# Weight block sums by accumulating DMAs in a seven-product feed-forward: two transformer blocks on one core

## What is computed

```python
def first_block(x, ...):
    ...
    x = x + jnp.einsum('btd,de->bte', mix, w_o[l])
    h = rmsnorm(x, ln2[l])
    gate, up = jnp.split(jnp.einsum('btd,df->btf', h, w_gu[l]), 2, axis=-1)
    x = x + jnp.einsum('btf,fd->btd', jax.nn.silu(gate) * up, w_down[l])
    return rmsnorm(x, ln_f)
```

## Time and profile before

| | us |
|---|---|
| three runs, median | 1124.53 (1123.28 to 1125.9) |
| the profiled execution | 1123.35 |
| its span, first to last instruction | 1121.5 |
| feed-forward, first gate matmul (228.80) to the end of the last down product (669.2) | 440.4 |

### The profile page before, as it was taken

One profiled execution on the slowest core, in us unless ns is written; L12 is line 12 of the kernel. 1 busy time (PEld: TensorE's weight loads), 2 busy tenths in 40 slices (PEclk: granted clock), 3 DMA queues, 4 the chain that ended last, 5 costly groups with the idle time before them and its releaser, 6 DMA issues.

```text
span 1121.5 us, 15711 instructions
## 1 busy us (share of the span) xinstructions
PE 1041.4 (93%) x5802; PEld 870.3 (78%) x5802; DVE 698.4 (62%) x1234; ACT 503.1 (45%) x945; POOL 486.8 (43%) x551
## 2 busy tenths in 40 slices
PE   9999999996777769998886999999999999999997
PEld 6887877775777768888886787876788777788886
DVE  6865666567566662346666685779965666425553
ACT  6432665543444442224444243645675555423333
POOL 1354533468566630046663343743353676541101
PEclk9999999997999999998888999999999999999999
DMA  8222332121222223312222333621132333233322
GB/s 281 87 76 76 96 88 84 57 77 37 76 76 76 75 90 117 94 58 75 75 76 76 113 102 104 222 77 57 58 88 83 95 113 113 75 95 94 94 75 75
DMA packets 34907, 102.51 MB, mean 91 GB/s; under 512 B 4608, under 2 KB 8128, under 8 KB 34832
## 3 DMA queue, kind: packets, MB, share of 16 engines
q1 hardware_dynamic: 34416, 100.99, 28.1%
q10 hardware_dynamic: 416, 0.52, 0.1%
HBM read 93.40 MB, written 4.74 MB: 88 GB/s over the span
## 4 chain that ended last, share of the span: by engine, by line
PE 64%; DVE 13%; POOL 9%; DMA 5%; issue 4%; ACT 4%; POOLq 0%; SPq 0%; DVEq 0%; ACTq 0%
PE bank L1684 16%; PE bank L1685 16%; PE bank L1686 16%; POOL WT L2629 8%; DMA WS<-wall 5%; PE bank L1848 2%; PE bank L1839 2%; DVE WL L2377 2%; DVE score L2490 1%; PE bank L1732 1%; PE bank L1734 1%; PE bank L1733 1%; DVE m L2488 1%; PE bank L1824 1%; ACT fs L2061 1%
## 5 line engine op out<-in xcount | busy, mean ns | idle before, releaser
L2580 POOL TENSOR_TENSOR WL<-WS,WH 128x256 fp32r<-128x256 f32 x272 | 219.8, 808 | 257.5 <-ACT WH L1901 240.4
L1684 PE MATMUL bank<-HH,WH 128*128 128x512 f32 x536 | 221.0, 412 | 10.1 <-DVE fa L2427 5.8
L1686 PE MATMUL bank<-HH,WL 128*128 128x512 f32 x536 | 211.6, 395 | 0.0
L1685 PE MATMUL bank<-HL,WH 128*128 128x512 f32 x536 | 211.4, 394 | 0.0
L1901 ACT ACTIVATE WH<-WS 128x1024 fp32r<-128x1024 f32 x122 | 126.4, 1047 | 36.6 <-PE bank L1686 34.5
L1698 PE MATMUL bank<-n_s,WH 128*128 128x256 f32 x304 | 92.4, 304 | 45.1 <-DVE WL L2377 33.8
L1684 PEld LDWEIGHTS bank<-HH,WH 128*128 128x128 f32 x536 | 102.5, 191 | 36.0 <-DVE fa L2427 6.2
L1686 PEld LDWEIGHTS bank<-HH,WL 128*128 128x128 f32 x536 | 101.9, 190 | 22.5
L1685 PEld LDWEIGHTS bank<-HL,WH 128*128 128x128 f32 x536 | 102.3, 191 | 19.2 <-issue 1.2
L2629 POOL TENSOR_TENSOR WT<-WS 128x256 f32<-128x256 f32 x76 | 68.2, 898 | 76.6 <-PE bank L1686 55.4
L1698 PEld LDWEIGHTS bank<-n_s,WH 128*128 128x128 f32 x304 | 60.9, 200 | 52.0 <-issue 33.7
(11 more groups left out here) (385 smaller groups left out, 2472.2 us busy)
## 6 DMA issues: line engine op xcount, KB each, us to landing
WS<-wall SPq DMA_DIRECT2D x161, 512.0 KB, 3.5
scratch<-rows SPq DMA_DIRECT2D x8, 320.0 KB, 5.1
b_t<-scratch SPq DMA_DIRECT2D x8, 256.0 KB, 3.6
X<-xT SPq DMA_DIRECT2D x7, 256.0 KB, 7.2
outT<-X SPq DMA_DIRECT2D x7, 256.0 KB, 2.4
b_m<-b_m SPq DMA_DIRECT2D x11, 128.0 KB, 2.2
f_s<-f_s SPq DMA_DIRECT2D x8, 128.0 KB
f_m<-f_m SPq DMA_DIRECT2D x8, 128.0 KB
```

The lines of the kernel that those rows point to most:

```text
L1684: e.matmul(b[:, :], wh, xh, start=k == 0, stop=False)
L1685: e.matmul(b[:, :], wh, xl, start=False, stop=False)
L1686: m = e.matmul(b[:, :], wl, xh, start=False, stop=k == n - 1)
L2580: e.tensor_tensor(WL[:, at_u, cs], WS[:, u % NST, cs], f32(WH[:, at_u, cs]), ALU.subtract).then_inc(*tick(w_low_g, u if c == 3 else (u, c)))
```

## The change

Four plain pairs instead of three, 18 pairs in the seven-product scheme instead of 19. The scheme is turned over (the roles of B11 and B22 change places): T1 = B22 + B12, T2 = T1 + B11, T4 = T2 + B21, T3 = B11 + B12. The sums are no longer made by POOL: a buffer `SS` of six blocks (128 x 512 each) is loaded by SP with B22, B11 and B21 from HBM (256 KB each, line 1627), and when a block's low half has been made, POOL issues a DMA (`b_add`, line 2682) that reads the next term from HBM and adds it into the same place in `SS`: B22 becomes T1, then T2, then T4; B11 becomes T3. That is three loads and four adding DMAs in each group; B11 and B12 are read from HBM twice. The `WS` ring now holds plain units alone, so units of the down product come in while the groups run. For plain pairs the low half of the weights moves from POOL to DVE (`now["low"] = w_low_g` goes). The product of gate and up in a group moves from POOL to DVE (`seven_mult`), and the `norm2` steps are spread one to a pair of tiles. `seven_step` puts steps of neighbouring groups beside each other: a group has places -9 to 12, the next begins seven places later, and each place has one of the seven products. The core of the diff:

```diff
-OLD_PAIRS = 3
+OLD_PAIRS = 4
+        SS = at("SS", [128, 6, 512], F32, place["at"])
-        WT = at("WT", [128, 2 * NW, 512], F32, WL_at)
...
-        def prepare(g, *names):
-            for name in names:
-                if name[-1] == "+":
-                    do("w_sum", g=g, name=name[:-1], before=block_at[g, name[:-1]][1])
-                else:
-                    do("w_block", g=g, name=name, before=block_at[g, name][1])
...
+        def make(g, name):
+            half = g[0]
+            while (g, name) not in block_at:
+                nxt = order_of[half].pop(0)
+                block_at[nxt] = slot(1, ("block", nxt))
+            do("w_block", g=g, name=name, before=block_at[g, name][1])
+            follower = {"B22": "T1", "T1": "T2", "T2": "T4", "B11": "T3"}.get(name)
+            if follower:
+                do("b_add", g=g, name=follower, after=name)
...
+        def group_at(g, x):
+            half, j = g
+            o = open_of.setdefault(g, {})
+            if x == -9:
+                do("b_load", g=g, name="B22")
+                do("b_load", g=g, name="B11")
+            elif x == -6:
+                make(g, "B11")
+            elif x == -5:
+                do("b_load", g=g, name="B21")
+            elif x == -4:
+                make(g, "B22")
+            elif x == -1:
+                make(g, "T1")
+            elif x == 0:
...
+                make(g, "B21")
+                o["yi"], o["y"], free = y_ring.take()
+                seven(g, "B11", "A11", o["y"], True, free)
+            elif x == 1:
+                do("partial", g=g, name="p", b=o["y"], dst=c_p)
+            elif x == 2:
+                make(g, "T2")
+                o["vi"], o["v"], free = t_ring.take()
+                seven(g, "B22", "s4", o["v"], True, free)
+            elif x == 3:
+                o["zi"], o["z"], free = s_ring.take()
+                seven(g, "T1", "s1", o["z"], True, free)
+            elif x == 4:
+                make(g, "T3")
+                seven(g, "T2", "s2", o["y"], False, partial((g, "p")))
+            elif x == 5:
+                do("partial", g=g, name="u2", b=o["y"], dst=c_u2)
+                make(g, "T4")
+                o["wi"], o["w"], free = t_ring.take()
+                seven(g, "B21", "A12", o["w"], True, free)
+            elif x == 6:
+                corner_of(g, "C11", o["w"], c_p)
+                t_ring.give(o["wi"], corner((g, "C11")))
+                seven(g, "T3", "s3", o["y"], False, partial((g, "u2")))
+            elif x == 7:
+                do("partial", g=g, name="u3", b=o["y"], dst=c_u3)
...
+            elif x == 8:
+                seven(g, "T4", "A22", o["z"], False, corner((g, "C22")))
+            elif x == 9:
+                corner_of(g, "C21", o["z"], c_u2)
...
+                do("seven_tanh", g=g)
+            elif x == 10:
+                do("seven_mult", g=g)
+            elif x == 11:
+                do("seven_hi", g=g)
+            elif x == 12:
+                do("seven_low", g=g)
...
-        now["low"] = w_low_g
...
+                elif kind == "b_load":
+                    g, name = s["g"], s["name"]
+                    n = groups.index(g)
+                    i = place_of(n, name)
+                    back, last = {"B22": (3, "T4"), "B11": (2, "T3"), "B21": (1, "B21")}[name]
+                    q.wait_ge(block_low((groups[n - back], last)) if n >= back else norm_a("n2"))
+                    e.dma_start(SS[:, i, :], wall_block(g, name)).then_inc(*block_in[i].tick((g, name)))
...
-                elif kind == "w_sum":
...
-                        e.tensor_tensor(WT[:, o, cs], src1[:, cs], src2[:, cs], ALU.add).then_inc(
-                            *tick(w_sum, (g, name) if c else (g, name, 0)))
+                elif kind == "b_add":
+                    g, name = s["g"], s["name"]
+                    i = place_of(groups.index(g), name)
+                    term = {"T1": "B12", "T2": "B11", "T4": "B21", "T3": "B12"}[name]
+                    q.wait_ge(block_low((g, s["after"])))
+                    e.dma_start(SS[:, i, :], wall_block(g, term), accum_op=ALU.add).then_inc(*block_sum[i].tick((g, name)))
```

More of the change, by code:

```diff
@@ L417, in tile @@
             plan.append(what)
-            while count["split"] <= min(t // UT + 2, NU - 1):
+            while count["split"] <= min(t // UT + 2, NU - 1) and not all(
+                    u in seven_of for u in range(count["split"], min(t // UT + 2, NU - 1) + 1)):
                 split()
@@ new lines, in seven_step @@
+        def seven_step(half, js, x):
+            if half not in order_of:
+                order_of[half] = [((half, j), name) for j in js for name in ("B11", "B22", "T1", "T2", "B21", "T3")]
+                for n, j in enumerate(js):
+                    order_of[half].insert(7 * n + (7 if n + 1 < len(js) else 6), ((half, j), "T4"))
+            for n in reversed(range(len(js))):
+                y = x - 7 * n
+                if y not in (7, 8):
+                    group_at((half, js[n]), y)
+                if n > 0 and y in (0, 1):
+                    group_at((half, js[n - 1]), y + 7)
@@ L1073, in build @@
                         next(up_gen)
-                    beside_old(gate_gen)
-                    beside_old(up_gen)
+                    for gen in (gate_gen, up_gen):
+                        for _ in gen:
+                            next(nh, None)
+                assert left == [0], left
                 run(nh)
-                js = js[OLD_PAIRS:]
-            now["low"] = w_low_v
-            for j in js:
-                seven_group((half, j), (half, j + 1) if j + 1 < FHS[half] else None)
+            js = of_half[half]
+            last = (half, js[-1])
+            for x in range(7 * len(js)):
+                seven_step(half, js, x)
+                if x == 7 * len(js) - 4 or x == 7 * len(js) - 1:
+                    split()
+            group_at(last, 7)
             if half == 1:
@@ L1509, in used @@
             return product_end(u) if kind == "block" else dense(unit_end.get(u, ("unit", u)))
[L1511 to L1518 removed]
+        plain = [u for u in range(NU) if u not in seven_of]
+        ring_of = {u: n % NST for n, u in enumerate(plain)}
+        groups = sorted(first_unit)
         def partial_free(g, name):
@@ L1550, in load @@
             def load(u):
-                while loads[0] <= min(u, NU - 1):
+                while loads[0] <= min(u, len(plain) - 1):
                     n = loads[0]
@@ L2055, in scalar_program @@
                     e.activation(NH[name][0][:, :, :].rearrange("p a n -> p (a n)"),
-                                 NF[:, NF_at[name]:NF_at[name] + 1024], ACT.Copy).then_inc(*norm2_a.tick(name))
+                                 NF[:, NF_at[name]:NF_at[name] + 1024], ACT.Copy,
+                                 scale=-1.0 if name == "A22" else 1.0).then_inc(*norm2_a.tick(name))
                 elif kind == "ffn_gate":
                     half, jj = s["half"], s["jj"]
-                    done = corner(((half, s["j"]), "C21")) if s["seven"] else out_v(("gate", jj))
```

318 lines of the change are left out of this document (142 added, 176 removed).

## The result

The changed kernel takes 1127.2 us (median of 13 runs, 1126.3 to 1129.1) where the kernel before takes 1124.05 in the same comparison: a ratio of 1.0030, 95% interval 1.0021 to 1.0038. It is a little slower. The prediction said 1092 and faster; the time lies in its range, on the other side of zero. The profiled execution has a span of 1126.9 us.

A forecast was written before the change was run, and what follows sets the result against it. Groups were bound by a ring of load, POOL sums, halves and load, 13.4 us each; the new ring costs 12.8. Front, groups, down products and seams end at 637.6 against 669.2: 31.6 less, 1091.8 us; range 1052 to 1136, forecast's own 1068 to 1119.

The forecast's parts named there:

- The loop: Group to group: T2's low half, C21, tanh, B22, T1, T2, two adds in series; 5.2 + 2A, 12.8 us.
- A: Time from a low half's end on DVE until ACT may read the adding DMA's sum; taken as 3.8 us.
- The second loop: Through tanh, two multiplications, result's high half and partial sum, one add: 8.3 + A; shorter once A is over 3.1.
- the prediction's own slope: Forecast total's change per microsecond of A: 2 + 16 x 2 = 34 us.
- The zero at A = 4.7: Value of A at which the forecast gain vanishes; above it the changed kernel would be slower.
- The rival with the slow add: At ACT's wait for `block_sum`: adding DMA slow; 1136 us at A of 5.1, 1167 at 6; chance 0.23.
- Sharing: Slow-add rival: T4's DMA, just ahead of T1's, shares the engines; forecast expected engines near 0.5 busy, added nothing.
- T4's add is hidden: Within a group: the DMA for T4, 4.7 us ahead of its reader, costs no time.
- The plain pairs: Stretch before the groups, DVE-bound: 38.3 us of work to 279.3; B22(0) done at 282.8, first T2 at 293.1.
- The seams: Waits into the down products, 4.29 and 5.75 us, go; 1.5 us left at each.
- T2 is on time: Second half's start: T2's chain of 10.3 us fits into 11.4 us, so T2 is ready at 479.1.
- PE's clock: No-change rival: PE at its lower clock eats the gain; 11.3 us a group, below 12.8; chance 0.04.

The follow-up runs named there:

- x2: Changed kernel with the adding DMAs as plain copies (sums left out), issued from SyncE's queue instead of GpSimd's: 1058.8 us.
- x1: Changed kernel with GpSimd's adding DMAs as plain copies of the same 256 KB, sums left out: 1077.7 us.
- x9: Changed kernel with the adds for T3 and T4, and from the fourth group the three loads, at 32 of 512 columns: 1108.0 us.
- x3: Changed kernel with the three plain loads of a group at 32 of 512 columns from the fourth group on: 1115.3 us.
- x5: Changed kernel with corner C21 and the tanh one place later, behind the making of B22: 1142.3 us, ratio 1.0171 to the kernel before.
- x7: Changed kernel with four places between each block of a pair's chain and its next: 1086.0 us, ratio 0.9668 to the kernel before.
- x13: x5 with the adds for T4 at 32 of 512 columns: 1124.6 us, ratio 1.0011 to the kernel before.
- x11: x7 with B11 made at place -2 instead of -6: 1090.4 us, ratio 0.9699 to the kernel before.

## Why the prediction failed, point by point

- **The loop** was right, step for step: C21, tanh, B22, T1, T2 as the chain has them. The formula 5.2 + 2A with the measured 4.2 and 5.4 gives 14.8 us; the trace has 14.58 in the round shown, and 14.3 as a mean of eight (T2's low half of the first pair starts at 295.52, of the ninth at 409.99). The second loop was right too, 8.3 + A, and x2 ran in it.
- **The size of A** is the step that failed. It was taken as 3.8, from plain loads of 256 and 512 KB (3.6 and 3.5), "and a little for the issue", with nothing for sharing. It is 4.2 and 5.4, a mean of 4.8. The runs take it apart: a plain copy from GpSimd's queue lands in 2.9 (x1); the adding brings it to 3.8 to 4.2 (x9); 0.28 lies between the low half and the issue; the loads beside it add some 0.9 to the second (x3). By the prediction's own slope, 34 us for 1 us of A, 1.0 us too little is 34 us: 1092 + 34 = 1126, and 1127 was measured (how much of this nearness is luck, the sum below says). The zero at A = 4.7 stood there as well. The Trainium skill, DMA: Bandwidth & Descriptors, section Anatomy of one DMA, led to an estimated 2.6 us, and the plain copies at 2.9 come near it; the adding ones do not.
- **Where the choice went wrong**: "an adding DMA brings 256 KB and reads as many back, so both resemble it". The rows were plain transfers; that an add asks for more than a plain one was said, and it was given no time. The engines' time doubles (10.6% of the span against 5.5% in x1). The rival with the slow add had the right place, ACT's wait for `block_sum`. Of its reasons the adding is borne out (x1), the sharing with T4's add is not. It had 0.23.
- **Sharing** was put down to T4's add ahead of T1's. In this order T4's add is 2.2 us ahead and costs T1's next to nothing; it was T2's that shared, with the loads (x3). Engines that were expected near 0.5 are busy 0.58.
- **T4's add is hidden**: right in this order, in which a corner and a tanh keep it and T1's apart. In x5, without them, it made T1's longer.
- **The plain pairs** were sized well: B11's low half starts at 280.25 (it was to follow 279.3), B22's ends at 283.5 (282.8). T2 of the first pair is ready at 296.2 instead of 293.1, and 2.4 of these 3.1 us are its two adds (4.14 and 5.83 in the chain, for 7.6 predicted).
- **The seams**: the two waits into the down products are gone, as said, and the products start early. "T2 is on time" in the second half was wrong; the timeline of PE, and below it the chain:

```profile
498.89 0.55 PE L1744 MATMUL bank<-n_s,WH 128*128 128x256 f32 x1 [4.29 <-DVE WL L2426]
```

```profile
490.32 0.69 DVE X L2415
491.01 0.61 DVE WL L2426
...
491.91 5.46 DMA SS<-wall
```

T1's add had landed at 489.08, but its low half stands in VectorE's queue behind the down product's last addition to `X`, which waits for the last wide matmul. That cost some 1.2 of the 3.1 us by which T2 is late, a wait that the prediction did not have; the rest is the add for T2, 5.46.

- **The sum**: the last down product ends at 673.1 instead of 637.6, 35.5 us late: 3.1 at the first T2, 12.1 in eight rounds of the first half, 1.5 to its down product's end, 3.1 at the second half's first T2, 14.1 in its eight rounds and 1.7 at the end, less rounding. Most of it is A. Over all sixteen rounds the adds give a mean A of 4.8 in the first half and 4.9 in the second; the excess over 3.8 makes 34 us, and the adds ahead of the two first T2s 4 more. The rounds' other steps gave 8 of these 38 back: 5.0 us instead of 5.2 in a usual round, and 2.7 in the first round of each half, where the chain goes from T2's low half straight to T1's add. Front, addition to `X`, seams and ends took 5. The 8 and the 5 nearly cancel, so that 1126 lies so near to 1127 is in part luck.
- **PE's clock**: granted 0.96 in both stretches of groups (0.99 and 0.90 before). PE is no member of the round in the chain above, so the clock does not set its length.

## What to carry to other kernels

A step that goes to an adding DMA is priced as a latency: where two stand in series in the loop that joins one tile to the next, their whole time counts, and moving the loop's members a place or two (x7) gained 41 us here, where taking 0.9 us of small steps out of the loop (x5) lost 15. When a sum is that steep in one unknown (34 us a microsecond), take the row nearest in kind, give what it lacks a price of its own, and let the range's far end weigh. Look at what a small step keeps apart before taking it out.

## What the runs showed of the hardware

- An adding DMA from GpSimd holds the DMA engines twice as long as a copy of the same bytes (10.6% of a span of 1126.9 us against 5.5% of 1075.6) and has 1.8 times the packets; its instruction holds GpSimd 877 ns against 541.
- A 256 KB add takes 3.7 to 4.4 us with next to nothing beside it (x9), 3.9 in the changed kernel behind another that was issued 2.2 us earlier (T4's at 354.22, T1's at 356.46), and more if it is issued closer behind another: 5.9 to 6.9 at 0.6 us (T1's in x5; 4.1 to 4.6 in x13, where that neighbour moves 16 KB), 5.1 to 6.4 at 1.2 us (T2's in x11, with two loads beside it).
